# A two-block decoder pass on one core: TensorE's multiplies into an unread bank, around every norm, are left out

## What is computed

```python
def _rmsnorm(x, g):
    y = xf * lax.rsqrt(jnp.mean(xf * xf, axis=-1, keepdims=True) + NORM_EPS)
    return (y * g.astype(jnp.float32)).astype(x.dtype)

for layer in range(DEPTH):                       # first block, DEPTH = 2
    h = _rmsnorm(x, norm_attn[layer])
    ...                                          # projections and attention
    x = x + mixed @ w_out[layer]
    h2 = _rmsnorm(x, norm_mlp[layer])
    x = x + jnp.square(jax.nn.relu(h2 @ w_up[layer])) @ w_down[layer]
x = _rmsnorm(x, final_norm)

for l in range(DEPTH):                           # second block
    x = layer_norm(ALPHA * x + 0.5 * swiglu(x, ...), ln_g[l, 0], ln_b[l, 0])
    ...                                          # y: pooling, convolution, neighbourhood attention
    x = layer_norm(ALPHA * x + y, ln_g[l, 1], ln_b[l, 1])
    x = layer_norm(ALPHA * x + 0.5 * swiglu(x, ...), ln_g[l, 2], ln_b[l, 2])
```

## Time and profile before

| what | value |
|---|---|
| median of 3 runs | 3363.25 us (3361.12 to 3364.02) |
| the profiled execution, its own time | 3359.27 us |
| its span in the profile | 3357.3 us |
| mean granted TensorE clock over it | 0.992 of full |
| TensorE busy | 3264.8 us, 97% of the span |
| VectorE busy | 2050.3 us, 61% |
| ScalarE, GpSimd busy | 21%, 9% |
| weights and all else moved by DMA | 302 MB, mean 90 GB/s |

### The profile page before, as it was taken

One profiled execution on the slowest core, in us unless ns is written; L12 is line 12 of the kernel. 1 busy time (PEld: TensorE's weight loads), 2 busy tenths in 40 slices (PEclk: granted clock), 3 DMA queues, 4 the chain that ended last, 5 costly groups with the idle time before them and its releaser, 6 DMA issues.

```text
span 3357.3 us, 44654 instructions
## 1 busy us (share of the span) xinstructions
PE 3264.8 (97%) x15358; PEld 2588.3 (77%) x15358; DVE 2050.3 (61%) x3166; ACT 715.4 (21%) x1419; POOL 288.7 (9%) x224
## 2 busy tenths in 40 slices
PE   8999999999999999999999999999999999999998
PEld 6766788878657888788886778888788877778886
DVE  5676655555776555654557776455745476774547
ACT  3465200014653000100003321000200023320001
POOL 0110100030101000200002410000100014200001
PEclk9999999999999999999999999999999999999999
DMA  5211222224112222223222123322222222222222
GB/s 217 92 45 51 91 94 100 94 76 151 39 55 75 94 100 94 88 95 101 94 88 94 64 70 100 100 94 88 93 96 94 96 68 97 67 88 99 95 95 68
DMA packets 86777, 302.20 MB, mean 90 GB/s; under 512 B 9267, under 2 KB 10035, under 8 KB 86368
## 3 DMA queue, kind: packets, MB, share of 16 engines
q1 hardware_dynamic: 81180, 287.67, 25.6%
q10 hardware_dynamic: 5444, 12.52, 1.1%
HBM read 298.03 MB, written 6.06 MB: 91 GB/s over the span
## 4 chain that ended last, share of the span: by engine, by line
PE 88%; DVE 5%; DVEq 3%; issue 2%; ACT 1%; DMA 1%; POOL 1%; POOLq 0%; ACTq 0%; SPq 0%
PE acc L534 19%; PE acc L533 19%; PE acc L532 19%; PE acc L630 3%; PE acc L631 2%; PE acc L632 2%; PE acc L879 2%; PE acc L881 2%; PE acc L880 2%; PE score L772 2%; PE outp L811 1%; PE trans L784 1%; DVE wL L1509 1%; PE acc L562 1%; DVEq L1508 1%
## 5 line engine op out<-in xcount | busy, mean ns | idle before, releaser
L1509 DVE TENSOR_TENSOR wL<-wraw,wH 128x1024 fp32r<-128x1024 f32 x459 | 605.2, 1318 | 34.3
L532 PE MATMUL acc<-opH,wH 128*128 128x512 f32 x1280 | 497.9, 389 | 0.0
L533 PE MATMUL acc<-opL,wH 128*128 128x512 f32 x1280 | 497.9, 389 | 0.0
L534 PE MATMUL acc<-opH,wL 128*128 128x512 f32 x1280 | 497.9, 389 | 0.0
L532 PE MATMUL acc<-hidH,wH 128*128 128x512 f32 x1072 | 417.0, 389 | 0.0
L533 PE MATMUL acc<-hidL,wH 128*128 128x512 f32 x1072 | 417.0, 389 | 0.0
L534 PE MATMUL acc<-hidH,wL 128*128 128x512 f32 x1072 | 417.0, 389 | 0.0
L1507 DVE CAST wH<-wraw 128x1024 fp32r<-128x1024 f32 x459 | 325.1, 708 | 135.3 <-PE acc L534 121.2
L1405 ACT ACTIVATE big<-acc 128x512 f32<-128x512 f32 x84 | 50.5, 601 | 1173.0 <-PE acc L534 1170.2
L533 PEld LDWEIGHTS acc<-opL,wH 128*128 128x128 f32 x1280 | 240.3, 188 | 50.0
L532 PEld LDWEIGHTS acc<-opH,wH 128*128 128x128 f32 x1280 | 240.3, 188 | 49.8
(11 more groups left out here) (310 smaller groups left out, 4949.7 us busy)
## 6 DMA issues: line engine op xcount, KB each, us to landing
wraw<-in_weights SPq DMA_DIRECT2D x507, 512.0 KB, 3.3
wraw<-in_weights SPq DMA_DIRECT2D x32, 384.0 KB, 3.0
big<-bias_scratch ACTq DMA_DIRECT2D x10, 512.0 KB, 3.6
bias_scratch<-bias_rows SPq DMA_DIRECT2D x3, 1280.0 KB
big<-in_par ACTq DMA_DIRECT2D x2, 1536.0 KB, 8.0
big<-in_x SPq DMA_DIRECT2D x4, 512.0 KB, 8.9
mixT<-bias_scratch ACTq DMA_DIRECT2D x2, 1024.0 KB, 7.6
out_x<-big SPq DMA_DIRECT2D x8, 256.0 KB, 2.3
```

Of the source, the lines that this page charges most:

```text
L532: pe.matmul(accum[:, :], wH[:, slot, w], hi[:, k, :], start=k == 0, stop=False)
L533: pe.matmul(accum[:, :], wH[:, slot, w], lo[:, k, :], start=False, stop=False)
L534: mm = pe.matmul(accum[:, :], wL[:, slot, w], hi[:, k, :], start=False, stop=k == n - 1)
L1509: dve.tensor_tensor(wL[:, slot, :], wraw[:, slot, :], wH[:, slot, :].bitcast(F32), ALU.subtract).then_inc(split_done, 1)
```

## The change

All calls of `keep_warm` and the function itself are taken out, with the parameter `rnd` that `norm` and `layer_norm` had for it. With the multiplies goes the wait for `split_done` ahead of them. The sums, the drains, the counts and all else stay.

```diff
-            def keep_warm(rnd, count):
-
-
-                pe.wait_ge(split_done, rnd * SLOTS + 1)
-                for _ in range(count):
-                    pe.matmul(spare[:, :], wH[:, 0, 0:P], wH[:, 0, 0:SEQ], start=True, stop=True)
-
-            def norm(n, rnd):
-                keep_warm(rnd, 12)
+            def norm(n):
                 settle(pe, (stat_ready, n))
                 pe.matmul(scp[0][:, :], ones, stat, start=True, stop=True).then_inc(summed, 1)
-                keep_warm(rnd, 13)
                 finish(pe, pe_end)
 
-            def layer_norm(m, rnd):
-                keep_warm(rnd, 8)
+            def layer_norm(m):
                 settle(pe, (ln_total, m * 2 + 1))
                 pe.matmul(scp[0][:, :], ones, stat, start=True, stop=True).then_inc(ln_summed, 1)
                 settle(pe, (ln_total, m * 2 + 2))
                 pe.matmul(scp[1][:, :], ones, square_sum, start=True, stop=True).then_inc(ln_var, 1)
-                keep_warm(rnd, 13)
                 finish(pe, pe_end)
...
             sum_x(3).then_inc(summed, 1)
-            keep_warm(0, 8)
             finish(pe, pe_end)
...
-                norm(layer * 2 + 2, layer * ROUNDS1 + ROUNDS1)
+                norm(layer * 2 + 2)
...
-                layer_norm(layer * 3, rounds + ROUND_NA)
+                layer_norm(layer * 3)
```

More of the change, by code:

```diff
@@ L1051, in _ @@
                     centred_group(d, rounds + ROUND_OUT2, gps + GP_OUT2, NC, opH, opL, layer * 3 + 1)
-                layer_norm(layer * 3 + 1, rounds + ROUND_FFN2)
+                layer_norm(layer * 3 + 1)
                 ffn(layer * SPLITS2 + (SPLIT_B2 + 2), rounds + ROUND_FFN2, gps + GP_FFN2, hids + sum(PARTS2),
                     layer * 3 + 2)
-                layer_norm(layer * 3 + 2, rounds + ROUNDS2)
+                layer_norm(layer * 3 + 2)
             for k in range(NC):
```

## The result

The changed kernel takes 3371.61 us (median of 11 runs, 3364.3 to 3375.54) against 3364.02 us of the kernel before in the same comparison: a ratio of 1.0022, with a 95% interval of 1.0014 to 1.0030, so +7.4 us. A second comparison on another occasion (6 runs of the changed kernel) gave 1.0033 (1.0021 to 1.0045), +11.1 us. The forecast was +7.15.

What follows compares the result with a forecast made beforehand. TensorE, busy 97% of the span, was taken to bound the kernel where it is late. 3.8 + 6.75 - 3.0 - 0.4 = +7.15 us on 3363.25 gave 3370.4 us, range 3364 to 3376.

Steps and rivals of the forecast that it cites:

- The 42 us are no gain: The 184 multiplies' 42 us of TensorE busy time stand nearly all in time it would have waited through.
- Half clock behind nearly every new gap: Gaps around norms and layer norms grow to about 3.1 to 4.7 us, so TensorE's clock halves behind nearly every one.
- Part 1: Sums of four layer norms and two norms run at half clock: 0.8 us each, +3.8 us new.
- Part 2: Products behind two norms and layer norms 1, 2, 4 begin at half clock: 1.35 us each, +6.75 us.
- part 4: At layer norm 2 the slowed thirteen multiplies no longer hold back the product: -0.4 us; everything else 0.
- The layer norms with two groups: Layer norms 0 and 3: products at half clock fall behind some 0.5 us and win it back: nothing lost.
- Part 3: End of layer 0: without thirteen multiplies TensorE reaches the jump to the loop's top earlier, -3.0 us.
- the end of layer 0 has its low stretch already, nothing new: Claimed no added half-clock cost for products at the end of layer 0, as the profiled run already had it.
- catching up: Rival: TensorE regains lost time because chunks come at VectorE's and ScalarE's pace; -3.4 to +3.5 us, chance 0.20.
- a jump bound by others: Rival: at the end of layer 0 another engine sets the jump's delay, no gain there; +10.2 us, chance 0.14.
- every low stretch costs in full: Rival: 11 more half-clock stretches at 1.6 us each, less 3.4; +14.2 us, chance 0.07.

Runs made afterwards that it cites:

- `all_but_first`: The kernel before, without only the 8 multiplies behind the first norm's sums: ratio 1.0003 (0.9994 to 1.0012).
- after: First profiled execution of the changed kernel, all 184 multiplies out, against the kernel before: span 16.3 us longer; timed ratio 1.0022.
- experiment 4: Took only the first norm's 8 multiplies from the kernel before: 1.0003; also compared the place at 90 across kernels' profiles.
- experiment 3: Against the kernel before: a norm's 13 multiplies behind its sum moved behind the layer loop, 0.9997; or 20 instead of 13, 3366.91 us.
- after again: The changed kernel once more, unchanged, with its own profile, against the kernel before: ratio 1.0033, +11.1 us; profiled span 17.4 us longer.
- `ahead_only`: The kernel before without the multiplies behind the sums and at the first norm; those ahead of the sums stay: 1.0015, +5.0 us.
- `more_in_loop`: The kernel before with 20 multiplies in place of 13 behind a norm's sum: one run, 3366.91 us.
- before: The kernel with all 184 multiplies, unchanged, profiled twice: median 3364.02 us in the first comparison, 3359.46 us when run again.
- `behind_only`: The kernel before without the multiplies ahead of the sums; those behind the sums and at the first norm stay: 1.0022, +7.4 us.

## Why the prediction was right, point by point

- **The 42 us are no gain**: held. TensorE's busy time fell by 15.5 us, and the span grew.
- **Half clock behind nearly every new gap**: held, with exceptions. 3.09 us left the clock full in `all_but_first` and lowered it in three other profiles; the 4.06 us ahead of a norm's sum left the sum itself at 1.10 us in two of four cases, the end of layer 0 in after being one, where the half clock began at the sum's end (720.9).
- **Part 1, the six sums**: +3.8. Measured 3.6 in both profiles.
- **Part 2, products at half clock**: +6.75, of which 1.35 at the first norm. The other four took 6.5 and 6.2 us, and the 0.4 that part 4 takes off at layer norm 2 is in these, so 1.7 each and not 1.35. The first norm lost 2.9 and 1.3, and by the places at 90 (experiment 4) this did not last, though no run isolates it. The prediction did not look on to the wait for weights 35 us later, and counted the 1.35 us as lasting. The layer norms with two groups lost nothing behind their sums, as said.
- **Part 3, the jump**: -3.0. The mechanism held (experiment 3): in after the product came 2.9 us earlier behind the sum's start, in after again 2.0, the sum being slow. Behind the sum the net was -1.55 and -1.4, as "the end of layer 0 has its low stretch already, nothing new" was wrong: the low stretch was 3.4 us before, of which 3.3 lay on products, and in after it lay on products from 725.1 to 731, twice as long. It cost 1.3 us more in after and 1.0 in after again.
- **The sum**: the places of the change, without the first norm, give 3.6 + 6.5 - 1.55 = 8.5 and 3.6 + 6.2 - 1.4 = 8.3 us. The medians say 7.4 and 11.1. The misses (+1.3 at four products, +1.5 at the jump, -1.35 at the first norm, -0.2 at the sums) come to +1.2, so the forecast is as near as it is because they nearly cancel. That the first median lies within 0.3 us of the forecast is luck: its interval is 4.7 to 10.1 us, and the second median misses by 4.
- **The rivals**: catching up falls with `ahead_only`; a jump bound by others falls with `more_in_loop`. That every low stretch costs in full, +14.2, is not excluded by the times alone, as the second comparison's interval reaches +15.1 and the pair of profiles differ by 16.3. The places decide it: layer norms 0 and 3 lost 0.0 us behind their sums, and the places of the change come to 8.5 and 8.3, or 11.4 and 9.6 with the first norm's loss, and not 14.2. By the Trainium skill, "TensorE: Matmul & The Clock Gate" (Terms), the penalty is about the throttled time times the missing share of the clock, for the 88 us an estimate of 44 us. The trace does not agree: the pair differ by 16.3 us, and from 720.90 to 724.30 it shows half clock with no multiply running at all.
- What the profiled pair adds to the places (the attention of layer 1, the gaps of 2.4 us) I did not forecast at all; at the gaps of 2.4 us before's profile has its clock full. Behind the two gaps of 2.4 us the clock fell in 12 of the 22 cases that the eleven profiles without fillers there give, in kernels with and without multiplies at the norms. But it fell in none of the four cases in the two profiles of before and in all four of after's, so whether the change moves these places, and part of the medians with them, stays open.

## What to carry to other kernels

Idle time of the bounding engine ahead of dense work had a second price behind it, about 1.7 us at each of the four product stretches here, and it was paid only where the engine was the late one afterwards. So count gaps, not removed instructions, and read at each what the work behind it waits for. Fillers should end before the real work is due, and are doubtful ahead of a jump or a drain on which the next stage stands; a filler that begins after the clock has fallen runs slow itself and can delay what it was to help, as in `behind_only`.

## What the runs showed of the hardware that I had not expected

- The gap of 1.91 us behind dense work lowered the clock in 13 of 22 cases (twice in each of eleven profiles), the one of 2.44 us in 12 of 22, and the one of 3.09 us left it full once in four. In this range the length of a gap alone does not tell. Ahead of the first sum of layer norms 0, 2, 3 and 5 the gap of 2.7 us was followed by a slow first or second sum in 12 of 24 cases (six profiles), the filled one of 0.9 us in none of 8.
- The same 184 multiplies cut to 32 columns each gave +10.4 us, no better than none. In its profile the clock stayed full at the first norm alone of the nine places.
- The way back to the top of the loop over the layers holds TensorE behind its drain: the branch record at the loop lasts 3.35 us in before and 3.44 us in after, against 0.07 and 0.08 us where the loop is left, and idle of 4.05 to 4.48 us stands ahead of the product in all twelve profiles, while all profiles but one put it down to a wait for `opH` that had long been served.
